# Normalisations of a two-block transformer kernel in halves of 512 features, and the first weight slots of a stage split ahead into places of their own

## The reference

```python
def _ffn_sublayer(h, mod, g_pre, g_post, w_in, w_out):
    shift, scale, gate = mod
    u = _modulate(_rmsnorm(h, g_pre), shift, scale)
    a, b = jnp.split(u @ w_in, 2, axis=-1)
    y = (jax.nn.silu(a) * b) @ w_out
    return h + MACARON_W * gate * _rmsnorm(y, g_post)
```

## Time and profile before

| | us |
|---|---|
| median of 3 runs | 3201.66 |
| lowest and highest | 3197.97, 3201.98 |
| the profiled execution | 3199.38 |
| its span | 3197.6 |
| PE busy | 2985.9 (93%) |
| DVE busy | 2032.8 (64%) |
| ACT busy | 1460.9 (46%) |
| POOL busy | 243.3 (8%) |
| mean granted TensorE clock | 0.968 |

### The profile page before, as it was taken

How to read it: one execution, slowest core, us unless ns; L and a number is a source line. 1 busy time by engine, 2 the same in 40 slices (tenths; PEclk the granted TensorE clock), 3 DMA queues, 4 the chain that set the end, 5 groups by cost and what they waited for, 6 DMA issues and landing times.

```text
span 3197.6 us, 36914 instructions
## 1 busy us (share of the span) xinstructions
PE 2985.9 (93%) x14616; PEld 2452.1 (77%) x14616; DVE 2032.8 (64%) x2475; ACT 1460.9 (46%) x1951; POOL 243.3 (8%) x182
## 2 busy tenths in 40 slices
PE   2999989878999999999899999998999999978999
PEld 1887878747887878888885788887588888976787
DVE  5778775686788787755536455544655454597654
ACT  3454453465454444545535444444444444444443
POOL 0000000000000000000400101000010100393100
PEclk9999999989999999999999999999599999989999
DMA  7767663204677777965530454554045455430453
GB/s 262 250 238 273 226 221 138 80 1 173 231 254 257 222 278 239 323 200 184 208 116 1 147 186 169 195 185 166 14 161 187 165 197 186 155 119 14 151 184 132
DMA packets 101546, 566.98 MB, mean 177 GB/s; under 512 B 20480, under 2 KB 20992, under 8 KB 44672
## 3 DMA queue, kind: packets, MB, share of 16 engines
q1 hardware_dynamic: 101376, 564.63, 51.0%
HBM read 563.50 MB, written 1.09 MB: 177 GB/s over the span
## 4 chain that ended last, share of the span: by engine, by line
PE 81%; DVE 11%; ACT 4%; issue 2%; DMA 2%; POOL 0%; SPq 0%; DVEq 0%; ACTq 0%
PE banks L336 23%; PE banks L338 23%; PE banks L337 23%; PE banks L1039 2%; DVE ada_terms L370 2%; PE banks L1062 2%; DVE w_rest L331 2%; PE banks L641 2%; PE banks L1047 1%; DMA ada_tiles<-in_w_ada 1%; DVE od_glu L1649 1%; DVE od_xbc L1690 1%; ACT w_high L320 1%; PE banks L1994 1%; PE banks L529 1%
## 5 line engine op out<-in xcount | busy, mean ns | idle before, releaser
L331 DVE TENSOR_TENSOR w_rest<-w_raw,w_high 128x2048 fp32r<-128x2048 f32 x430 | 988.5, 2301 | 576.3 <-ACT w_high L320 576.1
L320 ACT ACTIVATE w_high<-w_raw 128x2048 fp32r<-128x2048 f32 x440 | 838.0, 1908 | 325.1 <-PE banks L338 287.8
L336 PE MATMUL banks<-w_high,u_parts 128*128 128x512 f32 (+2 forms) x2272 | 871.3, 383 | 47.3 <-DVE post_term L472 23.3
L338 PE MATMUL banks<-w_high,u_parts 128*128 128x512 f32 (+2 forms) x2272 | 858.6, 378 | 0.0
L337 PE MATMUL banks<-w_rest,u_parts 128*128 128x512 f32 (+2 forms) x2272 | 857.1, 377 | 0.0
L336 PEld LDWEIGHTS banks<-w_high,u_parts 128*128 128x128 f32 x2272 | 432.7, 190 | 125.0 <-issue 50.6
L338 PEld LDWEIGHTS banks<-w_high,u_parts 128*128 128x128 f32 x2272 | 432.4, 190 | 79.7
L337 PEld LDWEIGHTS banks<-w_rest,u_parts 128*128 128x128 f32 x2272 | 433.3, 191 | 74.2
L336 PE MATMUL banks<-w_high,gated_high 128*128 128x512 f32 x968 | 379.0, 392 | 1.5 <-DVE w_rest L331 1.5
L338 PE MATMUL banks<-w_high,gated_rest 128*128 128x512 f32 x968 | 377.0, 389 | 0.0
L337 PE MATMUL banks<-w_rest,gated_high 128*128 128x512 f32 x968 | 376.7, 389 | 0.0
(11 more groups left out here) (216 smaller groups left out, 2874.6 us busy)
## 6 DMA issues: line engine op xcount, KB each, us to landing
w_raw<-in_w_ffn_in SPq DMA_DIRECT2D x242, 1024.0 KB, 4.9
w_raw<-in_w_ffn_out SPq DMA_DIRECT2D x121, 1024.0 KB, 4.9
ada_tiles<-in_w_ada SPq DMA_DIRECT2D x152, 512.0 KB, 5.4
w_raw<-in_w_mix SPq DMA_DIRECT2D x54, 1024.0 KB, 4.9
w_raw<-in_w_mix_out SPq DMA_DIRECT2D x22, 1024.0 KB, 4.9
post_gain_row<-post_mod SPq DMA_DIRECT2D x10, 512.0 KB, 6.4
na_bias<-in_na_bias SPq DMA_DIRECT2D x1, 4096.0 KB, 14.1
pre_gain_row<-in_gain SPq DMA_DIRECT2D x6, 512.0 KB, 7.6
```

Source lines behind the costliest of these rows:

```text
L320: act.activation(whi[:, g % RING, 0:n], raw[:, g % RING, 0:n], ACT.Copy).then_inc(w_hi_ready, 1)
L331: eng.tensor_tensor(wlo[:, g % RING, 0:n], raw[:, g % RING, 0:n], whi[:, g % RING, 0:n].bitcast(F32), ALU.subtract).then_inc(w_lo_by_pool ...
L336: nc.tensor.matmul(ps, hi_a, hi_b, start=first_, stop=False)
L338: return nc.tensor.matmul(ps, lo_a, hi_b, start=False, stop=last_)
```

## The change

The residual stream's two normalisations are cut in two halves of 512 features, and their arithmetic is put in another order. The gain row is multiplied to y before the root is known (`post_scale`), each half from its own PSUM bank; the squares of the two halves go to two columns, which VectorE adds (`post_average`); after the root one instruction per half multiplies and adds to the residual (`post_add`). Squares of the residual, `normed`, the transposes, the modulation and both parts of u also go by halves. In the first half-slots of an exposed feed-forward stage PE starts as soon as the high part of u is there, and does the pass with the rest afterwards.

The first two slots of each stage 5 to 11 get places outside the ring, in memory that is free at that time (`w_high_lead`, `w_rest_lead`), and are split, with the third slot, in the last part of `out_pe` (`split_upto`). GpSimd's splits and additions go to VectorE. The identity products are gone. Mixer 7 does its first two slots for tile 0 before tile 1 is turned; the load of its constants stands one slot earlier in SP's queue and waits until both slots are used, since the first lead place lies in the same memory.

The constants moved ahead of the sixth weight slot; the wait on `w_used` is now for two slots more. The core of the diff (of functions that are replaced whole only the new lines are shown; the old ones stand in the listing above):

```diff
+        lead_at = [mix_at + 49152, u_at + 2 * KT * SEQ * 4]
+        lead_hi = [place(f"w_high_lead{n}", [P, COLS], F32R, offset=lead_at[n]) for n in range(2)]
+        lead_lo = [place(f"w_rest_lead{n}", [P, COLS], F32R, offset=lead_at[n] + 4 * COLS) for n in range(2)]
...
+        begins = {s: first[f"in{s}x" if s in FFNS else f"in{s}"] for s in range(5, 12)}
+        lead_of = {begins[s] + n: n for s in begins for n in range(2)}
+        in_ring = [g for g in range(n_slots) if g not in lead_of]
+        ring_pos = {g: q for q, g in enumerate(in_ring)}
+        def w_high(g):
+            return lead_hi[lead_of[g]] if g in lead_of else whi[:, ring_pos[g] % RING]
+        def w_rest(g):
+            return lead_lo[lead_of[g]] if g in lead_of else wlo[:, ring_pos[g] % RING]
...
+            if g in lead_of:
+                name = next(m for m, _, _, n, _ in plan if m.startswith("out") and first[m] + n == g - lead_of[g])
+                act.wait_ge(w_used, first[name])
+            elif ring_pos[g] >= RING:
+                act.wait_ge(w_used, in_ring[ring_pos[g] - RING] + 1)
             n = slot_cols[g]
...
+        def split_upto(s, c, j):
+            name = f"out{s}{'xc'[c]}"
+            n, g = count_of[name], first[name] + j + LEAD
+            if s >= 4:
+                g = min(g + (j >= n - 3) + (j >= n - 2), first[name] + n + 2)
+            return g
...
+        def post_square(s, c, tt, half, wait_taken=False):
             act = nc.scalar
+            p = post_event(s, c, tt)
             await_y(act, s, c, tt)
+            if wait_taken:
+                act.wait_ge(y_taken, 2 * p + 1)
+            if tt:
+                act.wait_ge(post_summed, 2 * p + half - 1)
+            act.activation(junk[:, HALF[half]], y_pair(s, c, tt)[:, half], ACT.Square, scale=(2.0 if double(s) else 1.0) / 32,
+                           accum_out=post_col[:, half, p:p + 1]).then_inc(post_summed, 1)
...
+        def post_scale(s, c, tt, half, after_squares):
             dve = nc.vector
+            p = post_event(s, c, tt)
+            await_y(dve, s, c, tt)
+            dve.wait_ge(post_summed, 2 * p + after_squares)
             dve.wait_ge(post_gain_landed, 16 * (p // 2 + 1))
             if p:
+                dve.wait_ge(h_ready, 2 * p)
+            dve.tensor_tensor(t1[:, HALF[half]], y_pair(s, c, tt)[:, half], post_gain[:, HALF[half]], ALU.mult)\
+                .then_inc(y_taken, 1)
...
+        def post_average(s, c, tt):
+            dve = nc.vector
+            p = post_event(s, c, tt)
+            dve.wait_ge(post_summed, 2 * p + 2)
+            dve.tensor_scalar(post_col[:, 2, p:p + 1], post_col[:, 0, p:p + 1], post_col[:, 1, p:p + 1],
+                              (4.0 if double(s) else 1.0) * EPS, ALU.add, ALU.add).then_inc(post_mean, 1)
+        def post_take_root(s, c, tt):
+            act = nc.scalar
+            p = post_event(s, c, tt)
+            act.wait_ge(post_mean, p + 1)
+            act.activation(post_col[:, 3, p:p + 1], post_col[:, 2, p:p + 1], ACT.Sqrt).then_inc(post_root, 1)
+        def post_add(s, c, tt):
+            dve = nc.vector
+            p = post_event(s, c, tt)
+            dve.wait_ge(post_root, p + 1)
+            dve.reciprocal(post_col[:, 4, p:p + 1], post_col[:, 3, p:p + 1]).then_inc(post_inverse, 1)
             dve.wait_ge(post_inverse, p + 1)
+            dve.wait_ge(y_taken, 2 * p + 2)
+            for half in range(2):
+                hh = h[:, 2 * c + tt, HALF[half]]
+                dve.scalar_tensor_tensor(hh, t1[:, HALF[half]], post_col[:, 4, p:p + 1], hh, ALU.mult, ALU.add)\
+                    .then_inc(h_ready, 1)
+        def post_act(s, c):
+            for tt in range(2):
+                for half in range(2):
+                    post_square(s, c, tt, half)
+        def post_roots(s, c):
+            for tt in range(2):
+                post_take_root(s, c, tt)
+        def post_dve(s, c):
+            for tt in range(2):
+                for half in range(2):
+                    post_scale(s, c, tt, half, 2)
+                post_average(s, c, tt)
+                post_add(s, c, tt)
...
+        def stat_square(s, c, tt):
+            act = nc.scalar
+            e = pre_event(s, c, tt)
+            for half in range(2):
+                if s:
+                    act.wait_ge(h_ready, 2 * post_event(s - 1, c, tt) + half + 1)
+                else:
+                    act.wait_ge(in_landed[c], 16)
+                act.activation(junk[:, HALF[half]], h[:, 2 * c + tt, HALF[half]], ACT.Square, scale=1.0 / 32,
+                               accum_out=pre_col[:, half, e:e + 1]).then_inc(pre_summed, 1)
...
+            for half in range(2):
+                dst, src = xn[:, HALF[half]], h[:, 2 * c + tt, HALF[half]]
+                if s < 6:
+                    ins = dve.tensor_scalar(dst, src, pre_col[:, 4, e:e + 1], None, ALU.mult)
+                else:
+                    ins = dve.scalar_tensor_tensor(dst, src, pre_col[:, 4, e:e + 1], pre_gain[:, HALF[half]], ALU.mult,
+                                                   ALU.mult)
+                ins.then_inc(xn_ready, 1)
...
+            for half in range(2):
+                pe.wait_ge(xn_ready, 2 * e + half + 1)
+                for k in range(4):
+                    kt = 4 * half + k
+                    ins = pe.transpose(u_pair(s, c, tt)[:, half, k * P:(k + 1) * P], xn[:, kt * P:(kt + 1) * P], ident[:])
+                ins.then_inc(xn_turned, 1)
...
+                if f == 0 and exposed(s):
+                    pe.wait_ge(uhi_ready, 2 * pre_event(s, c, tt) + half + 1)
+                    for kt, w in kts:
+                        pe.matmul(ps, u[:, c, 0, kt, cols], hi[:, w], start=kt == 0, stop=False)
+                        pe.matmul(ps, u[:, c, 0, kt, cols], lo[:, w], start=False, stop=False)
+                    pe.wait_ge(u_ready, 2 * pre_event(s, c, tt) + half + 1)
+                    for kt, w in kts:
+                        ins = pe.matmul(ps, u[:, c, 1, kt, cols], hi[:, w], start=False, stop=kt == KT - 1)
+                else:
+                    for kt, w in kts:
+                        ins = three(ps, u[:, c, 0, kt, cols], hi[:, w], u[:, c, 1, kt, cols], lo[:, w], kt == 0,
+                                    kt == KT - 1)
...
-                keep_busy(bank[4], 8)
...
-        def keep_busy(ps, n):
-            for _ in range(n):
-                nc.tensor.matmul(ps[:, 0:P], ident[:], ident[:], start=True, stop=True)
...
         def hand_over_pe(s):
-            idle = bank[0 if s == 11 else 4]
-            keep_busy(idle, 20)
             turn_pe(s, 0, 0)
-            keep_busy(idle, 10)
-            if s not in FFNS:
+            if s == 10:
                 turn_pe(s, 0, 1)
         def hand_over_act(s):
-            post_act(s - 1, 0, 0)
-            if s in FFNS:
-                highs(first[f"in{s}x"] + 1)
+            post_square(s - 1, 0, 0, 0)
+            post_square(s - 1, 0, 0, 1, wait_taken=True)
+            post_take_root(s - 1, 0, 0)
             stat_act(s, 0, 0)
-            post_act(s - 1, 0, 1)
+            post_square(s - 1, 0, 1, 0)
             part_act(s, 0, 0)
-            if s in FFNS:
-                highs(first[f"in{s}x"] + 2)
+            post_square(s - 1, 0, 1, 1)
+            post_take_root(s - 1, 0, 1)
             stat_act(s, 0, 1)
+            part_act(s, 0, 1)
             if s in FFNS:
                 load_table(ACT.Silu)
-            part_act(s, 0, 1)
         def hand_over_dve(s):
-            post_dve(s - 1, 0, 0)
+            post_scale(s - 1, 0, 0, 1, 0)
+            post_scale(s - 1, 0, 0, 0, 1)
+            post_average(s - 1, 0, 0)
+            post_add(s - 1, 0, 0)
             stat_dve(s, 0, 0)
-            post_dve(s - 1, 0, 1)
             part_dve(s, 0, 0)
+            post_scale(s - 1, 0, 1, 0, 2)
+            post_scale(s - 1, 0, 1, 1, 2)
+            post_average(s - 1, 0, 1)
+            post_add(s - 1, 0, 1)
             stat_dve(s, 0, 1)
             part_dve(s, 0, 1)
...
-                    if e == 2 and self.s in (1, 4):
-                        pe.wait_ge(y_taken, 2 * PASSES.index((self.s - 1, 1)) + 2)
+                    if e == 2:
+                        pe.wait_ge(y_taken, 4 * PASSES.index((self.s - 1, 1 if self.s < 5 else 0)) + 4)
...
-                for c in range(6):
-                    self.proj.pe_chunk(c)
+                self.proj.pe_chunk(0, (0,))
+                self.proj.pe_chunk(1, (0,))
+                turn_pe(7, 0, 1)
+                self.proj.pe_chunk(0, (1,))
+                self.proj.pe_chunk(1, (1,))
+                for c in range(1, 6):
+                    if c > 1:
+                        self.proj.pe_chunk(c)
...
-        mixer_after = {first["in0c"] + 4: 1, first["v4x"] + AHEAD: 4, first["in7"] + AHEAD: 7, first["in10"] + AHEAD: 10}
+        mixer_after = {first["in0c"] + 4: 1, first["v4x"] + AHEAD: 4, first["in7"] + AHEAD - 1: 7, first["in10"] + AHEAD: 10}
...
 ```

(11 more changed lines are left out.)

292 lines of the change are left out of this document (118 added, 174 removed).

## The result

The changed kernel takes 3166.0 us (median of 4 runs, 3163.8 to 3167.7) against 3201.8 for the kernel before (4 runs, 3198.0 to 3214.5): ratio 0.9875, 95% interval 0.9856 to 0.9894. The forecast was 3163.0. Measured again on another chip, it took 3156.7 against 3195.5, ratio 0.9880. A profiled execution of it lasted 3166.3 us (span 3164.5).

What follows compares the result with a forecast made beforehand. TensorE was taken as the bound, busy 2985.9 of 3197.6 us, so gains lie only in its waits at the seams or in identities; the terms summed to 36.4 us, taking 3199.4 to 3163.0, own range 3156 to 3172, stated range 3144 to 3180.

Steps and rivals of the forecast that it cites:

- Hand-overs to 6, 8, 9, 11: Hand-overs into these stages: 4.4 us gained before tile 0's first product, 2.2 before tile 1's, less clock: 5.8 each, 23.2 together.
- delay by the third split: At these hand-overs, VectorE's rest of the next stage's third slot holds back its first product of y and gain 2.6 us.
- second gap: TensorE's stretch without products before tile 1's first product at a hand-over: 1.3 us where 3.5 stood, 2.2 gained.
- I charge half of 1.6 at each: Low-clock cost at each hand-over to 6, 8, 9, 11, after TensorE has nothing for 3.4 us; cuts 6.6 to 5.8.
- Stage 5: Hand-over to stage 5, same chain with modulation in halves: tile 1's first product at 23.8 us, before 32.7; 8.9 gained.
- Mixer 7: TensorE's wait for mixer 7's constants moves and does not vanish: +1 us gained, between +2 and -1.5.
- Mixer 10: Hand-over to mixer 10, whose first product needs both tiles: u of tile 1 complete at 19.8 us, before 18.4; loss 1.5.
- Mixers 1 and 4: TensorE's wait until y is read out of its banks gets shorter: 2.2 us gained at each, 4.4 together.
- Stages 0 to 3: Early stages: start +0.6 us, mixer 1 +2.2, stage 2 -0.9 because tile 0's chain waits for both roots.
- Rival (b): VectorE pays for work taken over in stages 0 to 4, eight passes at up to 3.2 us: 3185 us; chance 0.12.
- 2.75 is the product `normed` without GpSimd beside it: Share of the 4.4 us gained before tile 0's first product, hand-overs to 6, 8, 9, 11: `normed` without GpSimd's split beside it.
- the rest comes from halves: What remains of the 4.4 us: halves, the root off the path of y times gain, matmuls needing only the high part.

Runs made afterwards that it cites:

- e5_ids12: The changed kernel with 12 multiplications of the identity ahead of tile 0's transposes at each hand-over from stage 5 on; 3150.1 us, ratio 0.9837.
- e9_nopool: The kernel before, with VectorE instead of GpSimd making the rests of slots n + 1 and n + 2 at hand-overs into feed-forward stages; 3196.8 us, ratio 0.9999.
- e4_whole: The changed kernel with halves kept as instructions, but from stage 5 on every step waits for both halves; 3213.9 us, ratio 1.0028.
- e1_swap: The changed kernel with the two spare places holding slots n - 1 and n instead of n and n + 1; 3145.0 us, ratio 0.9814.

## Why the prediction came out right, step by step

The forecast's sum was 36.4 us, the medians give 35.8, the first profile's span 33.1. That the sum came so close is in part luck: two errors of opposite sign met. Up to the last product of stage 4 (at 1777.12 before, at 1770.50 and 1763.30 in the two executions) 4.1 us were forecast and 6.6 and 13.8 measured; behind it 32.3 were forecast and 26.5 and 26.1 measured. Term by term, gains in us, of the changed kernel's two profiles:

- **Hand-overs to 6, 8, 9, 11**: 23.2 forecast, 22.0 and 18.7 measured. The chain was right: delay by the third split 2.6 (2.4), first product +10.0 (+10.1), second gap from the first transpose to the product 1.3 (1984.01 - 1982.63 = 1.4). Mis-sized was "I charge half of 1.6 at each": the clock fell at seven of these eight, in the transposes or behind them, and cost 1.65 on average (28.1 us is a stretch at full clock; only the first one into 11 has it). With the whole 1.6 the term would have been 20.0; the mean of the two is 20.4. The Trainium skill (TensorE: Matmul & The Clock Gate, section Part 1) calls the throttled state the default. By that rule all four pay, and the trace agrees at seven of the eight; it was a better guide than halving between the two cases of the earlier trace rows.
- **Stage 5**: 8.9 forecast, 8.0 and 9.2.
- **Mixer 7**: +1.0 forecast, -0.5 and +0.5. That "the wait moves and does not vanish" held: 6.45 us in place of 6.30. The load is issued from 2184.59 on, when TensorE comes to wait for it, and its last part, issued at 2185.44, lands 5.5 us later, where 6.5 to 8.8 had been taken for the whole.
- **Mixer 10**: -1.5 forecast, -4.4 and -2.8. The gap grew by 2.6 us, from 13.3 to 16.0, and the clock is down in both sets of transposes (1.97 us for eight, after 3.17 and 6.97 of idling) and in the first product (0.55 against 0.35 in the earlier trace rows). What was left out is a price for the clock in this sum. With 12 identities in front of tile 0's transposes (`e5_ids12`) these take 1.32 us and the gap is 15.1, so 0.9 of the 2.6 hang on the clock there; the 1.7 left, near the 1.5 forecast, still hold tile 1's transposes at the low clock. Behind the first product the stretch is 1.7 and 0.3 us longer than before, and in `e9_nopool`, with the old code there, 1.5, so no run separates that part from the difference between executions.
- **Mixers 1 and 4**: 2.7 each at the wait (6.80 for 9.52 and 9.50), forecast 2.2 each.
- **Stages 0 to 3**: the last turned gate of stage 3 comes at 1473.9 and 1468.3 us, before at 1480.7 and, in `e9_nopool`, whose code is the same there, 1476.7. Over all nine executions with the changed code it lies between 1466.3 and 1475.6. Some 8 us gained, of which the forecast had 1.9 (mixer 1's 2.2 among them). TensorE's waits in this part, shown below the list, tell where they come from. Besides mixer 1's wait for `post_term` there were four more of 0.85 to 1.66 us, 4.2 together, which the forecast had not seen, and they are gone. The wait for u at the start is 1.2 us shorter (forecast 0.6), and that at stage 2 is 0.7 shorter (5.44 to 4.70), where the forecast had a loss of 0.9. With mixer 1's 2.7 that makes 8.8. Rival (b), VectorE paying for the additions, is out: TensorE's waits for `w_rest` up to there are 3.9 and 0.8 us, and were 1.6.
- **End of the kernel**: 0.7 forecast; from the last turned gate to the span's end it takes 61.7 us instead of 62.5.

TensorE's waits for VectorE to read y out of the banks in stages 0 to 3, first before, then changed (us in total, times, longest):

```profile
PE banks L336 <- DVE post_term L472: 13.8, 5, 9.5
PE banks L349 <- DVE post_term L490: 7.0, 2, 6.8
```

One attribution in the prediction does not stand, though it changed no number: "2.75 is the product `normed` without GpSimd beside it". Alone that edit gives 0.6 (`e9_nopool`), since the identities held TensorE anyway. And "the rest comes from halves" was in the prediction what remains of the 4.4 us, 2.35 (4.4 - 2.75 - 1.9 + 2.6). Without the overlap of halves the first gap is 9.35 us, as long as the 9.41 before, and the whole change is a loss (`e4_whole`): 47.9 us by the medians against the changed kernel's first 3166.0, some 1.5% by the ratios. So the prices of the parts do not add up: what one is worth hangs on which others are in place.

## What to carry to other kernels

Follow an early step to what its own input waits for: a third slot "split early" was bound by the place of its load and stood in the chain it was meant to clear; giving the spare places to the slots that free that place was worth 0.6%. Where TensorE's filler work is removed and gaps of about 3 us stay, charge the low clock in full at each (1.65 us here), and where filler is kept, size it again whenever the chain beside it gets shorter, since it then becomes the wait. Before handing VectorE's work to GpSimd, look which of VectorE's instructions in that time read two tensors from SBUF.

## What the hardware showed that I had not expected

- The clock's return differs from run to run of one kernel: at one hand-over a low stretch of 3.5 us in one execution and 6.8 in another, 29.4 against 30.7 us for the whole. It fell after 2.98 us of idling, and stayed at 1.00 after 0.71 and 0.30. Between, it went both ways: it stayed after 2.72 us (changed kernel, into 11) and fell after 2.65 (`e1_swap`, into 8). Behind mixer 4's waits of 6.8 and 2.1 us the granted clock of the same stretches was 0.80 and 0.78 in one run and 0.86 and 0.85 in another.
- VectorE's `residual` (two inputs from SBUF) took 2.5 us more than by itself, until a GpSimd instruction had ended, while `post_term` (one from PSUM) beside the same instruction took its usual 0.69.
